# The first three expert passes fetch their rows by token number, with more constant products ahead of the expert loop

## The reference, cut to what matters

```python
g_probs = softmax(t @ w_group); g_sel = argmax(g_probs); g_w = g_probs[g_sel]
e_logits = (t @ w_router)[group g_sel]              # 4 experts in the group
top_p, top_i = top_k(softmax(e_logits), 2)
weights = g_w * top_p / sum(top_p)
hid = silu(t @ w_gate[e]) * (t @ w_up[e])           # 16 experts, ff 256, two per token
y = sum over the two chosen e of weights[e] * (hid @ w_down[e])
```

## Time and profile before

| what | before |
|---|---|
| profiled execution, its own time | 1133.78 us |
| its span, first to last instruction | 1132.1 us, mean granted clock of TensorE 0.973 |
| PE busy | 1051.0 us (93%) |
| DVE, ACT, POOL busy | 446.2, 263.5, 241.0 us |
| chain that ended last | PE 78%, DVE 12%, DMA 3%, issue 3% |
| experts' passes, layer 0 / layer 1 | first `gate_up` at 539.04 / 959.06 us |

### The profile page before, as it was taken

How to read it: one execution, slowest core, us unless ns; L and a number is a source line. 1 busy time by engine, 2 the same in 40 slices (tenths; PEclk the granted TensorE clock), 3 DMA queues, 4 the chain that set the end, 5 groups by cost and what they waited for, 6 DMA issues and landing times.

```text
span 1132.1 us, 16440 instructions
## 1 busy us (share of the span) xinstructions
PE 1051.0 (93%) x6553; PEld 662.8 (59%) x6553; DVE 446.2 (39%) x806; ACT 263.5 (23%) x528; POOL 241.0 (21%) x232
## 2 busy tenths in 40 slices
PE   5999999999999999978999997989998978999993
PEld 4989979989988877753333332444444433333321
DVE  6400314224135541056223226657547745132217
ACT  5133143124224411020011111314214410011111
POOL 5333314305313534013000005510000012000004
PEclk8999999999999999998999999999999998999997
DMA  7232224115115111357799897130003058999955
GB/s 306 75 131 75 76 74 131 56 28 176 56 38 161 46 75 75 149 235 318 280 356 391 346 406 242 65 148 1 1 1 149 1 210 348 333 363 362 364 234 221
DMA packets 34838, 201.01 MB, mean 178 GB/s; under 512 B 4352, under 2 KB 4352, under 8 KB 25808
## 3 DMA queue, kind: packets, MB, share of 16 engines
q1 hardware_dynamic: 21168, 151.26, 35.2%
q10 hardware_dynamic: 8864, 31.74, 8.0%
q0 software_dynamic: 4736, 17.04, 4.0%
HBM read 303.70 MB, written 28.44 MB: 293 GB/s over the span
## 4 chain that ended last, share of the span: by engine, by line
PE 78%; DVE 12%; DMA 3%; issue 3%; ACT 2%; POOL 1%; SPq 0%; POOLq 0%; DVEq 0%; ACTq 0%
PE ps L844 31%; PE ps L1084 15%; PE ps L1104 7%; PE ps L969 4%; PE ps L1216 4%; PE ps L1158 3%; PE ps L850 3%; DVE arena L2095 2%; PE ps L1071 2%; DVE arena L2092 2%; PE ps L1060 1%; PE ps L912 1%; ACT arena L1534 1%; PE ps L1176 1%; DVE h L1955 1%
## 5 line engine op out<-in xcount | busy, mean ns | idle before, releaser
L844 PE MATMUL ps<-x_hi,ring_r 128*128 128x264 f32 x1024 | 191.7, 288 | 3.2 <-DVE xT L1574 3.1
L2174 POOL TENSOR_TENSOR ring_r<-ring,ring_r 128x1024 fp32r<-128x1024 f32 x56 | 137.0, 2459 | 261.2 <-ACT ring_r L1308 261.1
L844 PEld LDWEIGHTS ps<-x_hi,ring_r 128*128 128x128 f32 x1024 | 161.0, 190 | 3.7 <-issue 3.3
L1084 PE MATMUL ps<-arena,xT 128*32 128x512 f32 x864 | 158.8, 601 | 0.0
L1084 PE MATMUL ps<-ring,xT 128*32 128x512 f32 x672 | 144.7, 603 | 5.9 <-DVE xT L1574 5.9
L844 PE MATMUL ps<-xT_r,ring_r 128*128 128x264 f32 x512 | 146.7, 286 | 0.0
L1574 DVE TENSOR_TENSOR xT<-ps,gains 128x512 f32<-128x512 f32 (+1 forms) x76 | 46.9, 660 | 182.9 <-PE ps L1071 177.4
L844 PE MATMUL ps<-ring_r,x_hi 128*128 128x512 f32 x320 | 100.5, 395 | 0.0
L844 PEld LDWEIGHTS ps<-xT_r,ring_r 128*128 128x128 f32 x512 | 97.5, 190 | 0.1
L1104 PE MATMUL ps<-arena 128*32 128x512 f32 x624 | 90.4, 612 | 1.3 <-ACT arena L1445 1.3
L1308 ACT ACTIVATE ring_r<-ring 128x1024 fp32r<-128x1024 f32 x56 | 57.9, 1054 | 119.3 <-PE ps L844 70.8
(11 more groups left out here) (265 smaller groups left out, 1550.3 us busy)
## 6 DMA issues: line engine op xcount, KB each, us to landing
arena<-in_w_gu SPq DMA_DIRECT2D x22, 2048.0 KB, 14.7
ring<-in_w_gu SPq DMA_DIRECT2D x20, 2048.0 KB
arena<-in_w_down SPq DMA_DIRECT2D x36, 1024.0 KB
arena<-in_w_gu POOLq DMA_DIRECT2D x18, 2048.0 KB
ring<-in_w_gu POOLq DMA_DIRECT2D x14, 2048.0 KB
arena<-in_w_down POOLq DMA_DIRECT2D x26, 1024.0 KB
ring<-in_w_ret SPq DMA_DIRECT2D x48, 512.0 KB, 3.6
ring<-in_w_ret_out SPq DMA_DIRECT2D x16, 512.0 KB, 4.9
```

The costliest lines, as they stand in the source:

```text
L844: last = mm(dst, a_parts[x], b_parts[y], start=(start and n == 0), stop=(stop and n == 2))
L1084: last = mm(ps[cols, b, :], xgT[:, k % 2, c, cols], by_row(gu(j))[:, c, :], start=(c == 0), stop=(c == KT - 1))
L2174: G.tensor_tensor(w_lo[slot][:, m], w_raw[slot][:, m], w_hi[to][:, m], ALU.subtract).then_inc(lo_made, 1)
```

## The change

The normalized rows are also written to DRAM in token order (`token_rows`), by ScalarE's queue. VectorE works out the slots of pass 0 first, in a shorter chain that knows pairs only, and writes a one-hot matrix for it; then the half of `e_of` that holds the pairs (first `eb_ready`); then the rest of the slot chain, `slot_i`, and pass 1's one-hot matrix; then the rest of `e_of` (second `eb_ready`) and pass 2's one-hot matrix. For each of the three passes TensorE multiplies its one-hot matrix by a column of token numbers (`tokens_of`: 5 products with one column in layer 0, 4 in layer 1), ScalarE copies the 128 numbers as integers, and POOL gathers the rows of `token_rows` by them (`gather_rows`). The product of the one-hot matrix with `xn` and its copy are gone.

The places in the orders: on TensorE six constant products stand ahead of the mask product, seven ahead of `tokens_of(0)`, eight behind it and two behind `rows_to_features(0)` (23 in place of 9); `tokens_of(1)` stands in the middle of `gate_up(0)`, `tokens_of(2)` behind `rows_to_features(1)`. On POOL `gather_rows(0)` stands ahead of the scatters, `gather_rows(1)` behind the first six of them, `gather_rows(2)` behind all and ahead of the singles' register reads and loads. ScalarE takes pass 0's gain multiplication from VectorE, in 8 instructions. Slots 3 and 5 exchange their rooms: slot 5 is the one loaded after the scatters, and slot 3 is guessed. `w_q`'s first half, loaded during the passes before, is loaded together with the second after the loop.

```diff
-ROWS_SLOT = 3
-GUESSED = [4, 5, 0, 1, 2]
+ROWS_SLOT = 5
+GUESSED = [0, 1, 2, 3, 4]
+GATHERED = 3
...
-        one_hot = xg[:, 1, 0:640].rearrange("p (t s) -> p t s", t=5)
+        hot_in = (x_words[:, 3 * D:3 * D + 640], arena[:, LOGITS:LOGITS + 640], arena[:, LOGITS - 2 * D:LOGITS - 2 * D + 640])
+        one_hot = [x.rearrange("p (t s) -> p t s", t=5) for x in hot_in]
...
-        gat_at = {0: 14336, 1: 16384, 2: 27392, 3: 10240}
+        gat_at = {1: 16384, 2: 27392, 3: 10240}
+        gat = [down_rows if t == 0 else
...
+        token_rows = nc.dram_tensor("token_rows", (POS, D), F).ap()
...
-            return {0: ring[:, 0], 1: gu_arena[:, 0], 2: gu_arena[:, 1], 3: gu_rows, 4: ring[:, 1], 5: ring[:, 2]}[k % W_SLOTS]
+            return {0: ring[:, 0], 1: gu_arena[:, 0], 2: gu_arena[:, 1], 3: ring[:, 2], 4: ring[:, 1], 5: gu_rows}[k % W_SLOTS]
...
-                if k == last_use(5) + 1:
-                    sp.dma_start(ring[:, W_Q[0]], a["w_q"][0]).then_inc(q_in[0], 16)
...
-            sp.dma_start(ring[:, W_Q[1]], a["w_q"][1]).then_inc(q_in[1], 16)
+            for c in range(2):
+                sp.dma_start(ring[:, W_Q[c]], a["w_q"][c]).then_inc(q_in[c], 16)
...
+                def constant_products(n):
+                    for _ in range(n):
+                        mm(ps[:, B_YB, :], ident, con[:, 0:512], start=True, stop=True)
+                constant_products(6)
...
-                for _ in range(9):
-                    mm(ps[:, 4, :], ident, con[:, 0:512], start=True, stop=True)
-                pe.wait_ge(m["slot_ready"], 2)
-                for c in range(2):
+                def tokens_of(k):
+                    pe.wait_ge(hot_ready, GATHERED * l + k + 1)
                     for i, t in enumerate(tiles):
-                        last = mm(ps[:, c, :], one_hot[0:rows(t), t, :], xn[0:rows(t), t, 512 * c:512 * c + 512],
+                        last = mm(ps[:, B_TOKENS[k], 0:1], one_hot[k][0:rows(t), t, :], con[0:rows(t), C_TOKEN + t:C_TOKEN + t + 1],
-                last.then_inc(full[0], 1)
+                    last.then_inc(tokens_made, 1)
+                constant_products(7)
+                tokens_of(0)
+                constant_products(8)
...
+                    if k < GATHERED:
+                        pe.wait_ge(rows_gathered[k], 16 * (l + 1))
+                    else:
+                        pe.wait_ge(m[f"x_in{k % 2}"], rows_loaded(k))
                     if k:
-                        pe.wait_ge(m[f"x_in{k % 2}"], rows_loaded(k))
...
                     for c in blocks:
+                        if k == 0 and c == KT // 2:
+                            tokens_of(1)
...
                 rows_to_features(0)
+                constant_products(2)
                 gate_up(0)
                 rows_to_features(1)
+                tokens_of(2)
...
+                def store_rows(n):
+                    t = MOE_TILES[l][n]
+                    act.wait_ge(nrm[f"_m{l}"]["xn_done"], n + 1)
+                    act.dma_start(token_rows[128 * t:128 * t + rows(t), :], xn[0:rows(t), t, :]).then_inc(rows_stored, 16)
+                for n, t in enumerate(MOE_TILES[l]):
+                    squares(MOE_TILES[l], nrm[f"_m{l}"], moe_junk[l], ready, t)
+                    if n == 2:
+                        for early in range(3):
+                            store_rows(early)
+                for n, t in enumerate(MOE_TILES[l]):
+                    if n + 3 < len(MOE_TILES[l]):
+                        store_rows(n + 3)
...
-                fl.wait_full(act, f"X0_{l}")
-                nc.scalar.activation(xg[:, 0, :], flat(ps[:, 0:2, :]), ACT.Copy).then_inc(free[0], 1)
-                act.wait_ge(m["scattered"], 16 * 2 * (5 - l))
-                load_rows(1)
+                def tokens_of(k):
+                    act.wait_ge(tokens_made, GATHERED * l + k + 1)
+                    nc.scalar.activation(token_i[:, l, k:k + 1], ps[:, B_TOKENS[k], 0:1], ACT.Copy).then_inc(tokens_read, 1)
+                def first_features():
+                    round_full(act, l, B_ROWS, 0)
+                    for c in range(KT):
+                        last = nc.scalar.activation(xgT[:, 0, c, :], ps[:, c // 4, 128 * (c % 4):128 * (c % 4) + 128], ACT.Copy,
+                                                    scale=gains[:, G_MOE[l], c:c + 1])
+                    last.then_inc(free[B_ROWS], 1)
+                tokens_of(0)
+                first_features()
+                tokens_of(1)
                 tanh_of(0)
-                load_rows(2)
+                tokens_of(2)
                 for k in range(1, ROUNDS):
+                    if k == 1:
...
-                step.done(V_.tensor_reduce(v(N_, 16), passed, X, ALU.add))
...
+                def per_expert(x):
+                    return x.unsqueeze(1).to_broadcast([128, nt, 16])
+                fl.wait_read(dve, f"RK{l}")
+                step.done(V_.tensor_tensor(v(D_, 16), P1, P0, ALU.subtract))
+                step(V_.scalar_tensor_tensor(v(PC, nt, 16), per_expert(P0), float(PAIR), pos, ALU.mult, ALU.add))
+                step(V_.tensor_scalar(v(G64, 16), v(D_, 16), float(PAIR), None, ALU.mult))
+                step(V_.tensor_tensor(v(DBL, nt, 16), pos, per_expert(v(G64, 16)), ALU.is_ge))
+                step(V_.scalar_tensor_tensor(v(PC, nt, 16), v(DBL, nt, 16), float(ENC_D), v(PC, nt, 16), ALU.mult, ALU.add))
+                first_place, in_pairs = v(FIRST, 2, 5), v(CMP + 16 * THRESH, 2, nt, 16)
+                for n, at in enumerate((MA, MB)):
+                    step.done(V_.tensor_tensor(in_pairs[:, n], v(at, nt, 16), v(PC, nt, 16), ALU.mult))
+                step.wait()
+                for n in range(2):
+                    step.done(V_.tensor_reduce(first_place[:, n, 0:nt], in_pairs[:, n], X, ALU.add))
+                step.wait()
+                iota = con[:, C_IOTA:C_IOTA + 128]
+                def slots_of_pass(k, where, numbers):
+                    for t in range(nt):
+                        step.done(V_.tensor_scalar(one_hot[k][:, t, :], numbers, where[:, 0, t:t + 1], None, ALU.is_equal))
+                    step.wait()
+                    for t in range(nt):
+                        last = V_.scalar_tensor_tensor(one_hot[k][:, t, :], numbers, where[:, 1, t:t + 1], one_hot[k][:, t, :],
+                                                       ALU.is_equal, ALU.add)
+                    last.then_inc(hot_ready, 1)
+                slots_of_pass(0, first_place, iota)
+                eo, xo, dif, table = v(EO, 16), v(XO, 16), v(DIF, 16), v(ET, 4, 16)
+                step(V_.tensor_reduce(v(N_, 16), passed, X, ALU.add))
+                match = v(CMP, 16, 16)
+                shifted = v(SHIFT, 2, 5)
+                step.done(V_.tensor_scalar(shifted[:, :, 0:nt], first_place[:, :, 0:nt], -float(first_slot(2)), None, ALU.add))
+                step(V_.tensor_tensor(match, each16(P1), c16(num, 16), ALU.is_le))
+                step(V_.tensor_reduce(eo, match, X, ALU.add))
+                step.done(V_.tensor_scalar(table[:, 2, :], eo, float(EXPERTS), None, ALU.is_lt))
+                step.done(V_.tensor_scalar(table[:, 0, :], eo, float(EXPERTS - 1), None, ALU.min))
+                step(V_.tensor_tensor(v(OWN, W_SLOTS), eo[:, 0:W_SLOTS], num[:, 0:W_SLOTS], ALU.not_equal))
+                step(V_.tensor_tensor(table[:, 2, 0:ROWS_SLOT], table[:, 2, 0:ROWS_SLOT], v(OWN, W_SLOTS)[:, 0:ROWS_SLOT], ALU.mult))
+                V_.tensor_copy(e_of[:, l, 0:3:2, :], table[:, 0:3:2, :]).then_inc(m["eb_ready"], 1)
...
+                slots_of_pass(1, v(PLACE, 2, 5), con[:, C_SECOND:C_SECOND + 128])
...
-                V_.tensor_copy(e_of[:, l], table).then_inc(m["eb_ready"], 1)
+                V_.tensor_copy(e_of[:, l, 1:4:2, :], table[:, 1:4:2, :]).then_inc(m["eb_ready"], 1)
...
+                slots_of_pass(2, shifted, iota)
+                dve.wait_ge(hot_ready, GATHERED * (l + 1))
...
-                widen(0)
...
+                def gather_rows(k):
+                    pool.wait_ge(tokens_read, GATHERED * l + k + 1)
+                    if k == 0:
+                        pool.wait_ge(rows_stored, 16 * (5 * l + len(tiles)))
+                    if k == 2:
+                        round_full(pool, l, B_ROWS, 0)
+                    G.indirect_dma_start(xg[:, k % 2, :], None, token_rows,
+                                         bass.IndirectOffsetOnAxis(token_i[:, l, k:k + 1], 0)).then_inc(rows_gathered[k], 16)
...
+                def singles_step(k):
+                    if k == 0:
+                        pool.wait_ge(m["eb_ready"], 2)
+                    behind = chosen.pop()
+                    chosen.append({j: single_of(j) for kind, j in PASSES[k] if kind == "pair"})
+                    if chosen[0]:
...
+                gather_rows(0)
+                pool.wait_ge(m["slot_ready"], 1)
+                if l == 0:
+                    pool.wait_ge(s_zeroed, 32 * HEADS)
+                for n, t in enumerate(tiles):
```

(10 more changed lines are left out.)

104 lines of the change are left out of this document (41 added, 63 removed).

## The result

The changed kernel takes 1137.24 us (median of 7 runs, 1135.67 to 1138.81), the kernel before 1133.38 beside it: ratio 1.0035, 95% interval 1.0026 to 1.0044. It is slower by 0.35%, against 1138.4 us forecast (ratio 1.0041). The profiled execution took 1138.58 us for a span of 1136.8; that of before 1133.78 for 1132.1.

The account below looks back on a forecast made before the run. TensorE, busy 93%, bounds the kernel, so pass 1's `gate_up` start plus length counts: -0.7 + 1.5 in layer 0, +2.3 + 1.5 in layer 1, +4.6 on 1133.78 gives 1138.4 us. Range 1130.5 to 1144.

Parts of the forecast that it names:

- The ranking product: Mask product on TensorE: six constant products ahead keep the clock up, gaining 1.15 us in layer 0, 0.8 in layer 1.
- Pass 0's rows: Shorter slot chain and gather 0, landing in 6.5 us: `gate_up(0)` starts at 530.3 and 953.2, 8.7 and 5.9 us earlier.
- Edits at nothing: `token_rows` stores, memsets, later `w_q`, slot 5's load, more constants: each put at 0, bounds -0.5 and +1 us together.
- Pass 1's rows: Later `slot_i` and scatters; gather 1 at 535.9 and 959.45 lands in 5.8 us, TensorE waits 3.0 and 4.0, clock falls.
- rival 1: Clock still at 2.4 GHz when pass 1's transposes begin, no slow product: 1130.9 us; chance 0.22.
- The new chain: Copy 0.25, register reads 2.3, conditional loads 0.85 us behind `tokens_of(2)`: `gate_up(1)` starts at 549.4 and 972.3.
- The length of `gate_up(1)`: Pass 1's product starts at the lower clock, 8.60 against 7.07 us: 1.5 us more in each layer.
- Nothing later waits: Passes after pass 1: none waits for weights or rows it did not wait for before; otherwise the forecast is wrong.
- The rule of the Trainium skill: POOL's transfers: 2.0 us plus bytes at 436 GB/s, 3.2 us for 512 KB; by it the sum is about 1126.7 us.
- Rival 4: A gather lands as scatters do, in 3.5 us, and the clock holds: 1127.3 us; chance 0.06.

Follow-up runs that it names:

- before_const6: The kernel before with only six constant products added ahead of the mask product in both expert stages; ratio 1.0001 to the kernel before.
- fill_wait: The kernel after with four constant products added in the wait ahead of `gate_up(1)`; ratio 1.0036 to the kernel before.
- hold_downs: The kernel after with the guessed down loads of slots 2 to 4 issued only when gather 0 has landed; ratio 1.0092 to the kernel before.
- reads_first: The kernel after with the singles' four register reads moved ahead of the gather of pass 2; 1144.03 us, ratio 1.0052 to the kernel before.
- singles_first: The kernel after with `singles_step(0)` moved ahead of `gather_rows(2)` on POOL; total time not given, `gate_up(1)` at 41.8 and 40.6 us (kernel after: 43.1 and 43.5).
- after_again: The kernel after, unchanged, measured again on another chip; 1143.53 us, ratio 1.0043 to the kernel before.

## Why the prediction was right, and where it was not

The forecast's chain is the one that ran: pass 0 earlier, pass 1's `gate_up` behind a new chain of `tokens_of(2)`, its copy, register reads and conditional loads, and the lower clock on top. Forecast for the start of pass 1's `gate_up` and its length together: +0.8 us in layer 0 and +3.8 in layer 1; measured at pass 2's start -0.4 and +4.1. That the total came out at +3.9 us for +4.6 is in part luck, for several terms missed by 1 to 3 us with opposite signs, the last down product gave 1.7 us back, and 2.6 us came from outside the stages. Step by step:

- *The ranking product.* Clock 1.00 and 1.5 us: as said. That it is 1.15 us of gain I took for granted. before_const6 shows that by itself it was worth nothing in the time: in layer 0 the lower clock turned up in the next product. Nor is the gain always there. In five of the ten profiles of kernels that fetch rows by number the clock was down under the six constants of layer 0, and they held up the mask's product, which then ended 9.5 us after the logits' product started, as before (9.6), and not 8.4. fill_wait's constants, 7.09 us in place of 5.40:

```profile
502.84 7.09 PE L1061 MATMUL ps<-con 128*128 128x512 f32 x12
```

- *Pass 0's rows.* Layer 0: 530.72 against 530.3. Layer 1: 957.37 against 953.2. The term that failed is the landing of gather 0, 6.5 us forecast and 9.2 measured; the weights of slots 2 to 4 were still streaming, which hold_downs shows. Behind it the transposes ran at the lower clock (1.95 for 1.1 us), and the gather had left about half a us late. A part of this stands under *Edits at nothing*, where the stores were to move the end of the guessed weights by 1 to 3 us at no cost. The DMA engines were full 3.8 and 2.9 us longer, counted from the logits' product (to about 525.3 and 951.0, before 521.0 and 947.3), and gather 0 of layer 1 landed at 952.9, behind that end. The stores are the likely cause; no run separates them.
- *Pass 1's rows.* Scatter 1 at 528.76 and 951.66 (528.3 and 951.15), gather 1 at 536.24 (535.9). In layer 1 it left at 962.47, not 959.45, since `tokens_of(1)` stands in the middle of a pass 0 that was late; I had named that dependence for layer 0 only. Its landing was 5.8 us forecast, 4.6 and 4.5 measured, so TensorE waited 1.55 and 1.47 us, not 3.0 and 4.0, and the clock held ahead of the transposes. That is rival 1's condition, yet not its result: the clock fell a little later. In layer 0 it fell at about 542.8 (0.71 over 542 to 544), while `tokens_of(2)` still ran, and in layer 1 in the wait behind it.
- *The new chain.* From the end of `tokens_of(2)` to `gate_up(1)`: 4.3 us in layer 0 and 3.5 in layer 1, forecast 3.4. In layer 0 one of the reads took 1.10 us. The start came out at 547.55 (549.4) and 972.40 (972.3; its own terms add up to 972.45). In layer 1 that is luck: gather 1 left 3.0 us late, landed 1.3 sooner than forecast, and the transposes and `tokens_of(2)` took 1.7 less at the upper clock.
- *The length of `gate_up(1)`.* 1.5 us forecast, 2.7 and 1.9 measured. I had taken `gate_up(0)` of before, in which the clock came back some 3 us after the start (542:544 at 0.96); here it came back after 5 (552:554 at 0.73), and fill_wait shows that the whole excess is the clock's.
- *Nothing later waits.* A later pass that waits was one of my signs of being wrong, and it came true, at a small price in this kernel: in layer 1 pass 2's transposes waited 0.40 us for gather 2. Only the slow `gate_up(1)` hid the rest of it, 2.1 to 4.5 us in fill_wait, reads_first and singles_first. I had priced the last gather at nothing, and it stands beside slot 5's loads.
- *The rule of the Trainium skill* on POOL's transfers, page "DMA: Bandwidth & Descriptors", section "Anatomy of one DMA — SWDGE (gpsimd) path", gives an estimate of 3.2 us for 512 KB. This case's traces do not agree: no gather of rows landed under 4.3 us. Rival 4, which stood beside it, did not come.

Layer 0 was 183.4 us long in the first profile of the kernel after and 186.3 in the second, and the terms of that difference can be read. ScalarE's copy of the second column came 1.9 us later, and so did gather 1 and pass 1's transposes, by 1.8; the transposes and `tokens_of(2)` then ran at the lower clock, 1.7 us longer; the idle time ahead of `gate_up(1)` was 0.6 shorter (3.69 us): 2.9 in all. What stays open is what held up that copy, and what decides when the clock falls in layer 0.

## What to carry to other kernels

When a wait is taken from the path, look at what lands next and what is issued beside it: here four waits (register reads, gather 2, slot 5's loads, the clock) lay close together, and shortening the reads or the clock's price alone only handed over to the next. Move the producer ahead of a wait that exists anyway, and then fill what is left of the wait. At layer 1's pass 2 the first took 3.3 us off the loss and the second alone 0.9, the two together 5.0. A transfer on the path should not leave together with bulk loads, nor into a queue that still holds them; but a hold in front of those loads can push them onto the next transfer. And run the kernel before with the cheap part of a change alone: nine more constant products were worth as much as the best of the larger edits.

## What the runs showed of the hardware

- A skipped conditional load still stands on the path, yet it is cheap: `gate_up(1)` started 0.10 us after the second (547.45 to 547.55).
- Gather 0, an indirect gather of 512 KB, was issued into DMA engines that were full. In layer 0 they stayed full for some 5 us, and it landed after 5.2 to 6.8 us; in layer 1 for some 7 us, and it landed after 8.3 to 9.2. With 3 MB of this held back (hold_downs) it took 4.5 and 4.3.
- Gather 2 of layer 1 took 12.1 to 13.1 us in the five profiles in which slot 5's 3 MB were issued 0.4 and 1.1 us behind it, 4.6 to 5.0 where they came 2.5 to 2.6 us behind it, and 5.5 where they waited for it. What is issued later can thus delay a transfer by 8 us. It need not: in layer 0 of after_again and hold_downs the same loads were issued 0.7 and 1.3 us behind gather 2, and it landed after 5.0 and 6.5. What decides between the two stays open.
- In layer 0, ScalarE's copy of the second column of token numbers, which gather 1 waits for, started 0.04 us after its product in the first profile of the kernel after, and 1.3 to 2.1 us after it in the nine later profiles that have it, with nothing in the profile that released it then; in layer 1 it started within 0.4 us in all but hold_downs. The line is after_again's, whose product ended at 534.53:

```profile
536.49 0.17 ACT L1514 ACTIVATE token_i<-ps 128x1 int32<-128x1 f32 x1 [7.12 <-remote]
```
